# Norm factors made as 128x2 columns, tokens in the lanes, and spread by TensorE into PSUM

## What is computed

```python
def rmsnorm(x, g):                       # over the 1024 features of a token
    y = x * lax.rsqrt(jnp.mean(x * x, axis=-1, keepdims=True) + EPS)
    return y * g
def head_rmsnorm(o, g):                  # over the 256 features of a GLA head
    return o * lax.rsqrt(jnp.mean(o * o, axis=-1, keepdims=True) + EPS) * g
```

## Time and profile before

| | us |
|---|---|
| median of 3 runs | 1016.93 |
| lowest, highest | 1013.22, 1016.95 |
| the profiled execution | 1016.11 |
| its span, first to last instruction | 1013.6 |
| TensorE busy | 950.3 (94%) |
| VectorE busy | 800.7 (79%) |
| ScalarE busy | 556.3 (55%) |
| mean granted TensorE clock | 0.984 of 2.4 GHz |

### The profile page before, as it was taken

The page is one execution under the profiler, slowest core; times in us unless marked ns, Lnnn a source line. Parts: engine busy times, 40 slices in busy tenths (PEclk is TensorE's granted clock), DMA queues, the critical chain, the costliest instruction groups (busy, mean ns, idle before and its releaser), DMA issues.

```text
span 1013.6 us, 21553 instructions
## 1 busy us (share of the span) xinstructions
PE 950.3 (94%) x7406; PEld 923.2 (91%) x7406; DVE 800.7 (79%) x1313; ACT 556.3 (55%) x890; POOL 1.2 (0%) x6
## 2 busy tenths in 40 slices
PE   4899999999999997899999998999999889999995
PEld 4899999999999896899999997878799789999995
DVE  5998899998899785899998886856767777785543
ACT  5545666665545654676666555866432556664431
POOL 0000000000000000000000000000000000000000
PEclk9999999999999999999999999999999989999998
DMA  8677555555876563455555883654663437776551
GB/s 327 210 249 242 174 191 193 185 180 194 269 262 227 164 211 104 146 189 188 186 187 165 293 269 140 209 170 143 226 219 115 136 117 244 231 229 208 186 166 41
DMA packets 54453, 197.26 MB, mean 195 GB/s; under 512 B 6046, under 2 KB 7198, under 8 KB 54144
## 3 DMA queue, kind: packets, MB, share of 16 engines
q1 hardware_dynamic: 54256, 195.49, 58.8%
q10 hardware_dynamic: 144, 1.05, 0.3%
HBM read 195.46 MB, written 1.05 MB: 194 GB/s over the span
## 4 chain that ended last, share of the span: by engine, by line
PE 82%; DVE 10%; ACT 4%; DMA 2%; issue 2%; DVEq 0%; ACTq 0%; SPq 0%
PE ps L413 23%; PE ps L414 23%; PE ps L415 23%; DVE wlo L1257 3%; DMA raw<-stream 1%; ACT whi L801 1%; PE ps L443 1%; PE ps L445 1%; PE ps L444 1%; DVE rstd L1284 1%; PE ps L459 1%; DVE raw L1339 1%; PE ps L395 1%; DMA ct<-cst 1%; PE ps L396 1%
## 5 line engine op out<-in xcount | busy, mean ns | idle before, releaser
L1257 DVE TENSOR_TENSOR wlo<-raw,whi 128x1024 fp32r<-128x1024 f32 x306 | 371.8, 1221 | 86.2 <-ACT whi L801 85.6
L413 PE MATMUL ps<-xhi,whi 128*128 128x256 f32 x1288 | 365.9, 284 | 19.2 <-DVE wlo L1257 16.2
L801 ACT ACTIVATE whi<-raw 128x1024 fp32r<-128x1024 f32 x306 | 321.3, 1054 | 112.3 <-DMA raw<-stream 61.3
L414 PE MATMUL ps<-xlo,whi 128*128 128x256 f32 x1288 | 363.0, 282 | 0.0
L415 PE MATMUL ps<-xhi,wlo 128*128 128x256 f32 x1288 | 362.9, 282 | 0.0
L413 PEld LDWEIGHTS ps<-xhi,whi 128*128 128x128 f32 x1288 | 244.7, 190 | 20.7 <-issue 15.6
L414 PEld LDWEIGHTS ps<-xlo,whi 128*128 128x128 f32 x1288 | 244.7, 190 | 0.7 <-issue 0.5
L415 PEld LDWEIGHTS ps<-xhi,wlo 128*128 128x128 f32 x1288 | 244.7, 190 | 0.0
L413 PE MATMUL ps<-yhi,whi 128*128 128x256 f32 x400 | 112.5, 281 | 3.0 <-DVE ylo L1366 3.0
L415 PE MATMUL ps<-yhi,wlo 128*128 128x256 f32 x400 | 112.3, 281 | 0.0
L414 PE MATMUL ps<-ylo,whi 128*128 128x256 f32 x400 | 112.3, 281 | 0.0
(11 more groups left out here) (274 smaller groups left out, 1447.7 us busy)
## 6 DMA issues: line engine op xcount, KB each, us to landing
raw<-stream SPq DMA_DIRECT2D x362, 512.0 KB, 4.1
h<-xT SPq DMA_DIRECT2D x1, 1024.0 KB, 4.9
c<-ctxT ACTq DMA_DIRECT2D x1, 1024.0 KB, 6.3
out<-h SPq DMA_DIRECT2D x8, 128.0 KB, 2.1
ct<-cst SPq DMA_DIRECT2D x1, 962.5 KB, 7.3
rt_tab<-rot SPq DMA_DIRECT2D x1, 896.0 KB
cr<-crow SPq DMA_DIRECT2D x1, 512.0 KB, 11.0
state<-crow SPq DMA_DIRECT2D x1, 512.0 KB, 12.2
```

The costliest lines, as they stand in the source:

```text
L413: pe.matmul(dst, whi[:, w], at(hi, k), start=(k == 0), stop=False)
L414: pe.matmul(dst, whi[:, w], at(lo, k), start=False, stop=False)
L801: c.sig(act.activation(whi[:, s * D:(s + 1) * D], raw[:, r * D:(r + 1) * D], ACT.Copy), hi_ready)
L1257: c.sig(dve.tensor_tensor(wlo[:, w], raw[:, r], whi[:, w], ALU.subtract), slots_done)
```

## The change

The sum of squares is now made with the squares as the stationary operand and a single column of ones as the moving one, once for each half of 128 tokens. That leaves one column of 128 tokens in the lanes for each half, in `COLS`. Root and reciprocal run on 128x2 (`sqrt_columns`, `reciprocal_columns`). `spread` then multiplies the column, broadcast over 128 columns as the stationary operand, with the identity, which puts the factor of each token in all lanes of a bank again. The readers take it from PSUM (`RSTD`, or `ps[3]` for the heads); two factors that are needed long after, the context's and the first stage's, are copied to SBUF by ScalarE. The six other factors keep their form.

Beside it: for the heads the product of head 2 and 3 (`head_product`) stands ahead of the norm before it on VectorE, ahead of the MLP `resid` is written out twice and its last square is not added by VectorE but summed by TensorE as a second piece, and GpSimd's two memsets wait for a later signal.

```diff
+        COLS, factors, RSTD = STAT[:, 3 * P:3 * P + 4], spare[:, 4:8], STAT[:, 0:T]
+        first_rstd = sq[:, T:2 * T]
...
-            pool.wait_ge(ev("first_stat"), 1)
+            pool.wait_ge(ev("first_spread"), 1)
...
+            def column_stat(pieces, sides=None, at_col=0):
+                for tk in range(2):
+                    for k, piece in enumerate(pieces):
+                        last = pe.matmul(COLS[:, at_col + tk:at_col + tk + 1], piece[:, tk * P:(tk + 1) * P],
+                                         (ones if sides is None else sides[k])[:, 0:1], start=(k == 0),
+                                         stop=(k == len(pieces) - 1))
+                return last
...
+            def spread_to(bank, at_col=0):
+                for tk in range(2):
+                    last = pe.matmul(bank[:, tk * P:(tk + 1) * P], factors[:, at_col + tk:at_col + tk + 1].to_broadcast([P, P]),
+                                     ident, start=True, stop=True)
+                return last
+            def spread(bank=STAT):
+                pe.wait_ge(rstd_ready, c.n["stat_ready"])
+                c.sig(spread_to(bank), ev("spread"))
...
-            stat_of([csq_c[:, 0:T], csq_c[:, T:2 * T]])
+            column_stat_of([csq_c[:, 0:T], csq_c[:, T:2 * T]])
             out_chunk(7)
             tile[0] += 2
-            units(DC - 2, DC, ohi, olo)
+            units(1, DC, ohi, olo)
+            spread()
+            units(DC - 3, DC, ohi, olo)
...
-            pe.matmul(STAT[:, 0:T], ones, ssum[:, T:2 * T], start=True, stop=False)
-            c.sig(pe.matmul(STAT[:, 0:T], cst_of("eps"), ssum[:, 0:T], start=False, stop=True), stat_ready)
-            pe.matmul(ps[7][:, 0:T], ones, ssum[:, 0:T], start=True, stop=True).then_inc(ev("first_stat"), 1)
+            column_stat([ssum[:, 0:T]], at_col=2)
+            c.sig(column_stat([ssum[:, T:2 * T], ssum[:, 0:T]], [ones, cst_of("eps")]), stat_ready)
             pe.wait_ge(ev("tables_late"), 32)
+            def both_spread():
+                spread()
+                spread_to(ps[7], 2).then_inc(ev("first_spread"), 1)
...
-                   {0: lambda: gate_logits(0, 0), 3: lambda: gate_logits(0, 1)}, n_tiles=2)
+                   {0: lambda: (both_spread(), gate_logits(0, 0)), 3: lambda: gate_logits(0, 1)}, n_tiles=2)
...
             gla_stat(0)
             gla_values(2)
+            pe.wait_ge(ev("gla_masked"), GH)
+            spread(ps[3])
             gla_stat(1)
             gla_values(3)
+            def next_spread(hd):
+                pe.wait_ge(y_f32, 2 * hd)
+                spread(ps[3])
+            next_spread(1)
             gla_out_chunks(0, 2)
             gla_stat(2)
             gla_out_chunks(2, 4)
+            next_spread(2)
             gla_stat(3)
-            gla_out_chunks(4, DC)
+            gla_out_chunks(4, 6)
+            next_spread(3)
+            gla_out_chunks(6, DC)
             units(DC - 2, DC, zhi, zlo)
-            stat()
+            c.take(ssum_ready, 7)
+            pe.wait_ge(ev("n2_square"), 1)
+            column_stat_of([ssum[:, 0:T], at(sq, 1)])
+            spread()
...
+            def sqrt_columns(n, eps=EPS):
...
+                c.sig(act.activation(root[:, 0:2], COLS[:, 0:2], ACT.Sqrt, scale=1.0 / n, bias=eps), root_ready)
...
-            sqrt_stat(D)
+            sqrt_columns(D)
             c.n["tile_read"] += 8 + 4
+            act.wait_ge(ev("spread"), 1)
+            act.activation(rstd_c[:, :], RSTD, ACT.Copy).then_inc(ev("ctx_rstd"), 1)
...
+            act.wait_ge(ev("first_spread"), 1)
+            act.activation(first_rstd, ps[7][:, 0:T], ACT.Copy).then_inc(ev("first_kept"), 1)
...
+            def reciprocal_columns(n=2):
+                c.take(root_ready)
+                c.sig(dve.reciprocal(factors[:, 0:n], root[:, 0:n]), rstd_ready)
...
-            reciprocal_root(rstd_c)
+            reciprocal_columns()
...
-            reciprocal_root(rstd)
+            dve.wait_ge(ev("first_root"), 1)
+            reciprocal_columns(4)
+            c.take(ev("spread"), 2)
             modulated(h, 0, 0, xlo, (3, 5, 8))
             lo()
-            dve.wait_ge(ev("first_root"), 1)
-            link(dve.reciprocal(first_rstd, at(sq, 0)))
+            dve.wait_ge(ev("first_kept"), 1)
...
             def head_norm(hd):
-                reciprocal_root(rstd)
                 dve.wait_ge(ev("gla_read"), hd + 1)
+                c.take(ev("spread"))
...
-                    c.sig(dve.tensor_tensor(at(rsil, k), at(rsil, k), rstd[:, :], ALU.mult), y_f32)
+                    c.sig(dve.tensor_tensor(at(rsil, k), at(rsil, k), ps[3][:, 0:T], ALU.mult), y_f32)
...
             for hd in range(GH):
+                reciprocal_columns()
+                if hd + 1 < GH and hd:
+                    head_product(hd + 1)
                 head_norm(hd)
-                if hd + 2 < GH:
-                    head_product(hd + 2)
...
-            resid(1, None, gate=2 * DC)
-            reciprocal_root(rstd)
+            resid(1, None, gate=2 * DC, last_square=True)
+            reciprocal_columns()
+            c.take(ev("spread"))
             modulated(h, DC, 3 * DC, xlo)
```

More of the change, by code:

```diff
@@ L464, in stat, with column_stat_of @@
                 stat_of([ssum[:, 0:T]])
+            def column_stat(pieces, sides=None, at_col=0):
[5 more added lines that the diff above has]
+                return last
+            def column_stat_of(pieces):
+                c.n["root_ready"] = c.n.get("stat_ready", 0)
+                c.again(root_ready)
+                c.sig(column_stat(pieces), stat_ready)
+            def spread_to(bank, at_col=0):
[6 more added lines that the diff above has]
+                c.sig(spread_to(bank), ev("spread"))
             pe.wait_ge(ev("tables"), 32)
@@ L773, in _ @@
             looped(DC // 2, 8, MC, mhi, mlo, lag=2, final=c.n["y_ready"])
-            stat()
+            c.take(ssum_ready, 8)
+            column_stat_of([ssum[:, 0:T]])
+            spread()
         @block.scalar
@@ L816, in sqrt_stat @@
                 c.sig(act.activation(root[:, :], STAT[:, 0:T], ACT.Sqrt, scale=1.0 / n, bias=eps), root_ready)
+            def sqrt_columns(n, eps=EPS):
+                c.n["rstd_ready"] = c.n.get("root_ready", 0)
+                c.again(rstd_ready)
+                c.take(stat_ready)
+                c.sig(act.activation(root[:, 0:2], COLS[:, 0:2], ACT.Sqrt, scale=1.0 / n, bias=eps), root_ready)
             def ffn_up(conv):
@@ L852, in ffn_up, with resid @@
                 c.sig(act.activation(at(yhi, FC - 1), at(prod, 1), ACT.Copy), yhi_ready)
-            def resid(units_per, gain, gained=None, beside_ctx=False, ahead=False):
+            def resid(units_per, gain, gained=None, beside_ctx=False, ahead=False, last_square=None):
                 per = {hi_ready: 4 * units_per, tile_read: 4, sq_ready: 8 if gained else 4}
@@ L876, in four @@
                                                  scale=vt[:, bass.ds(i * 4 + (VEC[gain][0] + m), 1)]), xhi_ready)
+                        if last_square and m == 3 and i == 1:
+                            act.wait_ge(ssum_ready, c.value(sq_ready, -1))
+                            act.activation(at(sq, 1), at(h, DC - 1), ACT.Square).then_inc(ev(last_square), 1)
+                            continue
                         square(h, i * 4 + m, 0 if gained else m)
@@ L879, in four @@
                             square(h, i * 4 + m, 1, vt_col(i * 4 + (VEC[gained][0] + m)))
-                if ahead:
+                if ahead or last_square:
                     four(0)
@@ L1114, in _ @@
             hi()
-            sqrt_stat(D, EPS * EPS)
-            act.wait_ge(ev("first_stat"), 1)
-            act.activation(at(sq, 0), ps[7][:, 0:T], ACT.Sqrt, scale=1.0 / D, bias=EPS).then_inc(ev("first_root"), 1)
+            sqrt_columns(D, EPS * EPS)
+            act.activation(root[:, 2:4], COLS[:, 2:4], ACT.Sqrt, scale=1.0 / D, bias=EPS).then_inc(ev("first_root"), 1)
             gate_parts(0, 0)
@@ L1397, in resid @@
             def resid(units_per, gain, gate=None, gained=False, ada_from=None, ada_ctx=True, beside_ctx=False, ada_ms=(0, 1, 2, 3),
-                      ahead=False):
+                      ahead=False, last_square=False):
                 clear_sum()
@@ L1457, in four @@
                             finish(m - 1)
-                        if m == 3:
+                        if m == 3 and not (last_square and i == 1):
                             finish(3)
@@ L1863, in _ @@
             mlp_down(DC - 2)
-            reciprocal_root(rstd)
+            reciprocal_columns()
+            c.take(ev("spread"))
             for k in range(DC):
-                dve.scalar_tensor_tensor(out=at(h, k), in0=at(h, k), scalar=col("g_fin2", k), in1=rstd[:, :],
+                dve.scalar_tensor_tensor(out=at(h, k), in0=at(h, k), scalar=col("g_fin2", k), in1=RSTD,
                                          op0=ALU.mult, op1=ALU.mult).then_inc(ev("out_chunk"), 1)
```

15 lines of the change are left out of this document (9 added, 6 removed).

## The result

The changed kernel takes 1019.01 us (median of 20 runs) where the kernel before takes 1015.88, a ratio of 1.0026 with a 95% interval of 1.0014 to 1.0038: 2.6 us slower (1.4 to 3.9). The medians alone differ by 3.1; the ratio is taken from the fast executions only, so it leaves out two slow ones of the kernel before, of 2628 and 4772 us. The profiled execution took 1019.09 us with a span of 1017.3, against 1016.11 and 1013.6. So the forecast of 1017.5 was right in kind (within 0.5% of the kernel before) and 1.5 us low, and the 2.6 us were to be explained: the forecast had 0.6.

A forecast was written before the change was run, and what follows sets the result against it. TensorE, busy 94% of the span, was taken as the bound, so only its waits and own work count. Terms 2.1 + 0.9 + 0.6 - 1.2 - 0.8 - 1.0 = +0.6 us took 1016.93 to 1017.5; range 1013.0 to 1020.5.

The forecast's parts named there:

- context, to the restart: Context norm beside the attention's output: ScalarE's wait for the spread moves TensorE's restart by +2.1 us, pause becomes 4.8.
- context, clock behind it: After the context norm's pause: no added cost from the low clock in the forecast; a rival put a second slow stretch there.
- entry: Entry of the second stage: two spreads, eight passes ahead of the gate logits, delay the chain behind by +0.9 us.
- heads: Norm factors of the four heads: spreads in TensorE's queue outweigh the 1.6 us saved, +0.6 us.
- MLP, to the first chunk: Norm ahead of the MLP: addition gone, root and reciprocal shorter, spread added, square perhaps sooner: -1.2 us.
- MLP, clock behind it: Chunks behind the MLP norm: shorter pauses let the low clock end about 818 instead of 821.3, gaining 0.8 us.
- last norm: Last norm, from the sum to the first product: 2.0 us instead of 3.0, so -1.0 us.
- the likeliest case: The forecast itself, whole kernel: +0.6 us, to 1017.5 us, chance 0.52.
- the rival: Context norm: longer pause brings a second slow stretch, costing half of 3.3 us more, 1019.2 us; chance 0.18.
- its other case: Last norm with the clock low by then: the gain would be 0.6 us instead of 1.0.
- One-column passes near 0.11: TensorE's sums made as columns: each one-column pass takes 0.11 us; rival of twice that, 1025.2 us, chance 0.05.
- PSUM reads cost nothing: Readers of a spread: VectorE product from PSUM 480 ns, from SBUF 479; rival of dearer reads, 1018.2 us, chance 0.05.

The follow-up runs named there:

- the two repaired kernels: Changed kernel, ScalarE's context wait later, entry spreads behind first gate logits; last head's spread one chunk earlier (1012.23 us, 0.9961) or heads as before (1010.92 us, 0.9962).
- the profile with the wait moved: Changed kernel with ScalarE's wait for the spread and its context-factor copy moved behind the two small copies and the gate-weight copy: 1013.69 us, ratio 0.9972.

## Why the prediction was right or wrong, point by point

| term | forecast | measured | |
|---|---|---|---|
| context, to the restart | +2.1 | +2.2 | 10.52 to 12.74 |
| context, clock behind it | 0 (rival: +1.7) | +1.2, an estimate | PEclk 0.80 to 0.65 over 8 us, means of four and five profiles |
| entry | +0.9 | +0.9 | 4.05 to 4.93 |
| heads | +0.6 | +0.9 | 18.16 to 19.07 |
| MLP, to the first chunk | -1.2 | -1.3 | 6.50 to 5.18 |
| MLP, clock behind it | -0.8 | 0 | eight chunks 8.0 us, as before |
| last norm | -1.0 | -1.1 | 4.45 to 3.33 |
| sum | +0.6 | +2.8 | the ratio says +2.6, between 1.4 and 3.9 |

- *Context: right.* The spread started at 403.23 and was read at 403.87, 0.64 later (0.44 + 0.17 + 0.09 had been forecast), and VectorE's step came 2.2 us later, as worked out. ScalarE's wait and what stood behind it were named; moving the wait gave back 2.9.
- *Context, clock: the likeliest case missed it, the rival had it nearer.* The forecast took the slow stretch to end as it did in the profile of before, at 3.3 us. That profile was a middling draw: its second showed none, and with the longer pause all five show some 6.8 us. The rival put 1.7 on it, half a second stretch; against the mean of the old draws it is 1.2 by the profiles, and the clocks of whole executions leave open whether it is that much. That the rival's 1019.2 lies beside the measured 1019.01 is in part luck: it keeps the forecast's 0.8 of gain ahead of the MLP, which did not come.
- *Entry: right*, by the eight passes, 629.49 to 630.50 at the weight loads, and all of it reached the restart.
- *Heads: mechanism right, size 0.3 short.* The pauses shrink from 3.09 to 2.19 and the four spreads add 1.8. The 0.3 is missed ahead of the third head's chunks, which come 15.44 us behind the first sum for 14.80, 0.6 later where 0.4 was forecast; from there to the fourth head's it is 0.26 more, against 0.24. The sums are not the cause. The rows of the weight loads and of the third head, kernel before, then changed:

```profile
772.17 0.73 PEld L459 LDWEIGHTS ps<-osq,ct 128*128 128x128 f32 x4
773.36 0.41 PEld L709 LDWEIGHTS ps<-qf,state 128*128 128x128 f32 x2
...
784.51 0.74 PEld L459 LDWEIGHTS ps<-osq,ct 128*128 128x128 f32 x4
```

```profile
777.91 0.97 PEld L472 LDWEIGHTS ps<-ct,osq 128*128 128x128 f32 x8
...
779.13 0.41 PEld L743 LDWEIGHTS ps<-qf,state 128*128 128x128 f32 x2
...
791.24 0.53 PEld L485 LDWEIGHTS ps<-ct,spare 128*128 128x128 f32 x4
791.36 0.60 PE L485 MATMUL ps<-ct,spare 128*128 128x128 f32 x4
792.07 0.75 DVE L1866 TENSOR_TENSOR rsil<-rsil,ps 128x256 f32<-128x256 f32 x2 [0.83 <-PE ps L485]
```

A sum and the pair of matmuls behind it take 1.22 us (777.91 to 779.13) for 1.19 (772.17 to 773.36), no difference, as forecast. The mis-sized term is the spread. The two earlier ones move the third's place by 0.99 us (13.33 behind the first sum's weight load, for 12.34) where 0.90 was put down. And from the third's own weight load to its reader it is 0.83 us (791.24 to 792.07), where the forecast had 0.65: it counted from the weight load at 784.5 and not from the first matmul, 0.12 later, and left little for the signal.

- *MLP, clock: wrong.* The gain of 0.8 rested on low time being tied to the pause's end. In the changed kernel the low stretch began 1.7 us ahead of the first chunk and lasted 5.1 us into the chunks; before it was 1.7 and 5.2. In nine profiles with the short chain the eight chunks take 7.2 to 8.4 us, 8.0 in the mean, and 8.0 to 8.2 in three with the long one.
- *Last norm: right*, and its other case, a gain of 0.6 with the clock low by then, is what the two repaired kernels and the one with only the last two places show (3.83 us).
- *One-column passes near 0.11: right.* Twelve take 1.34 us (weight loads from 625.48 to 626.82), 0.112 each; four spread passes 0.45 to 0.55. *PSUM reads cost nothing: right.* `a` from PSUM takes 475 ns in the mean, not more than the 479 from SBUF; the sixteen readings:

```profile
L1738 DVE SCALAR_TENSOR_TENSOR a<-h,gmod,ps 128x256 f32<-128x256 f32 x16 | 7.3, 475 | 3.6 <-PE ps L485 3.6
```

The Trainium skill, "VectorE: DVE Perf Modes", section "The TRN2 errata", gives a PSUM source a larger fixed cost than SBUF; for this form the trace does not show it.

The range held. What was missed was 0.8 us that the clock ahead of the MLP did not give back, up to 1.2 at the context norm, and the heads' 0.3. The 1.5 us between forecast and median are smaller than the scatter of the kernel before, so the agreement of the total shows little; the places show the mechanism.

## What to carry to other kernels

A value that goes over one more engine is late by that engine's queue and not by its own work: here a factor was ready 1.9 us earlier, and the work behind ScalarE's wait for its spread came 2.2 us later. Look first at what stands behind the new wait on the waiting engine; if nobody needs the value soon, put the wait behind what others do need (one moved copy turned a loss of 2.2 us into a gain of 0.7). And make such a change place by place: five places under one idea were worth +2.2, +0.9, +0.9, -1.3 and -1.1, and the two good ones alone gave a kernel that is faster by 0.4%, with an interval of 0.2 to 0.6.

## What the runs showed that was not expected

TensorE's back-to-back matmuls of 256 columns keep one of three spacings, 117.3, 118.7 or 120.0 ns, for a hundred microseconds and more at a granted clock of 1.00, and change to another where TensorE has paused or where a norm's sum breaks its stream (at 114 us in the profile with the wait moved, without a pause). In the first profile of before the spacing goes from 117.3 to 118.7 ns at 549 us and again at 910, and in that of the changed kernel from 118.7 to 117.3 at 577. The timelines of TensorE there, two of before and one of the changed kernel:

```profile
549.30 0.39 PE L413 MATMUL ps<-yhi,whi 128*128 128x256 f32 x1 [1.52 <-DVE ylo L1366]
...
910.47 0.38 PE L413 MATMUL ps<-mhi,whi 128*128 128x256 f32 x1 [1.65 <-DVE mlo L1832]
```

```profile
576.92 0.38 PE L415 MATMUL ps<-yhi,whi 128*128 128x256 f32 x1 [0.37 <-DVE wlo L1321]
```

The same kernel shows different ones in different executions, though not everywhere: from 799 to 806 us all twelve profiles show 120.0. Over some 700 us of such stream one step is 1.2%, up to 8 us. It explains why the first two profiles, of the kernel before and of the changed one, drifted apart by 1.6 us between 419 and 564 us (117.3 against 118.7), in code that was not touched, and it is one likely reason, not varied in any run, why executions of one kernel spread over 1010 to 1020 us. The granted clock is another: among the changed kernel's first 20 executions its mean goes from 0.980 to 0.987, which is 7 us of the span, and the slower ones have the lower clock (correlation -0.77). What sets the spacing was not found. A difference of 2 us between two profiles is therefore nothing until the places are measured from their own starts.
